# A hybrid two-layer model on one core: the RWKV-7 recurrence in four chunks of 64 steps instead of two of 128

## The chip, the cores and the metric

The kernel runs on one core of one Trainium2 chip. The metric is the device time of one execution in microseconds (us), of which the median of several runs is taken. All arithmetic is fp32. Engines: PE (TensorE matmul; PEld is its weight load), DVE (VectorE), ACT (ScalarE), POOL (GpSimd), SP (SyncE, which here only issues DMAs).

## The reference, cut to what matters

256 tokens of width 1024 pass an even layer (RG-LRU and RWKV-7 side by side, then an FFN), an odd layer (mLSTM, then a mixture of 8 experts) and a final norm. The change lies in the RWKV-7 part, with 8 heads of 64:

```python
def step(state, inp):
    r_t, w_t, k_t, v_t, kk_t, a_t = inp
    sa = einsum('bhvk,bhk->bhv', state, -kk_t)
    state = (state * w_t[:, :, None, :] + sa[..., None] * (kk_t * a_t)[:, :, None, :]
             + v_t[..., None] * k_t[:, :, None, :])
    return state, einsum('bhvk,bhk->bhv', state, r_t)
```

It also moves parts of the RG-LRU (a conv of width 4, two sigmoid gates, tanh and square root, a linear scan) which is computed beside it.

## The kernel before, in words

The order on every engine is written out by hand; engines wait on counting semaphores. The projections of layer 0 come as 11 pairs of 128 columns, `project(0)` to `project(10)`, 32 matmuls of 128x128x256 in records of two per product, into PSUM banks 0 to 3 in turn; each waits until ACT (`shifted`, or copies of lru_x and the gate) and DVE (`shift`) have emptied its bank. Between them stand small groups on PE: `z_done` (decay), `kk_sum` (norm of k), `am_done` (a), `g_done` (gate).

The recurrence is chunked: for each chunk and head the steps of a chunk are related by a triangular matrix, whose inverse is built by doubling. The head dimension is 64, so a group of 128 rows of a tile `j` (four of them) holds two heads; `q` counts chunk and head parity, so that (q, j) are the 16 pairs of chunk and head. In order on PE:

- `transposed`: V, then the LRU's gate products, then B and K, turned through PE and emptied by ACT.
- pairwise products: for each q, K and B (64 rows of 128) against AR (A and R side by side, 256 columns), and A against B: 48 products. DVE masks them into NR, RBt, XT, X and M.
- levels 1 to 6: Z = M XT for each (q, j), ACT empties Z, then X Z and Z X; DVE merges both into XT and X by a masked copy (`copy_predicated`, L1364 and L1367). All tiles 128x128. After each level DVE does one part of the LRU (`lru(lv)`, L1343 to L1358).
- chunk steps: values (nv), U, state ST, output y; chunk 1 waits for the state of chunk 0.

Then `project_out` begins with the LRU's half of the output projection, followed by the layer norm of y. `Em` and `Ep` are decay factors, from scans of `sg` (Gp), by 16 exponentials on ACT. Constants: `cf` (fp32 matrices) gates the first matmul, `lm` (masks, loaded as fp32 and cast by POOL). The FFN weights are fetched once y is done.

## Time and profile before

| | us |
|---|---|
| median of 3 runs | 1499.72 (1496.15 to 1500.17) |
| the profiled execution | 1502.07 |
| its span, first to last instruction | 1500.3 |
| PE busy, share of the span | 1418.1 (95%) |
| PEld busy | 887.5 (59%) |
| DVE, ACT busy | 326.2 (22%), 181.1 (12%) |

A profile records one execution. A busy PE is not a PE at its peak, for its records overlap and its clock has two levels: the granted clock (PEclk) is 1.00 at 2.4 GHz and 0.50 at 1.2 GHz. In shapes, "64*128 64x256" is a matmul that uses 64 rows and 128 columns of the array, with a moving operand of 64 partitions by 256 columns. The chain of work that ended last is what sets the time; a share on it says little about what a part would give if it were shorter, since another wait may end later.

### The profile page before, as it was taken

What the parts mean: (1) busy time and instruction counts of PE and PEld (TensorE: products, weight loads), DVE (VectorE), ACT (ScalarE), POOL (GpSimd) and SP (SyncE); (2) the same over time, 40 slices, a digit from 0 to 9 for tenths busy, and PEclk for the clock granted to TensorE, in tenths of its full rate; (3) what the DMA queues carried; (4) which work ended last, traced back from release to release, by engine and by line L of the source; (5) the groups of instructions that cost most, each with busy time, mean ns of one, the idle gap of its engine ahead of it and who ended that gap; (6) DMA issues with size and microseconds to landing.
All of it is one profiled execution on the core that took longest, in us unless ns stands there. A gap on an engine that the chain in (4) does not pass through costs nothing.

```text
span 1500.3 us, 25303 instructions
## 1 busy us (share of the span) xinstructions
PE 1418.1 (95%) x11796; PEld 887.5 (59%) x11796; DVE 326.2 (22%) x603; ACT 181.1 (12%) x380; POOL 12.9 (1%) x23
## 2 busy tenths in 40 slices
PE   6999999899999989979799999999999999999995
PEld 5787996688888868758454344343443434434332
DVE  2364650500000062484200000010100101001012
ACT  2242211100000023230111000000000000000001
POOL 0010000000000000000000000000000000000000
PEclk9995996999999999798899999999999999999998
DMA  9400000593610270324378999999999999999742
GB/s 361 162 0 0 1 2 0 188 349 128 219 43 1 84 298 13 141 116 176 110 287 325 388 396 361 402 376 391 391 360 395 369 398 386 371 392 359 299 151 91
DMA packets 72913, 348.03 MB, mean 232 GB/s; under 512 B 5720, under 2 KB 13144, under 8 KB 56160
## 3 DMA queue, kind: packets, MB, share of 16 engines
q1 hardware_dynamic: 72496, 345.33, 59.4%
q8 instruction: 94, 1.54, 0.4%
q10 hardware_dynamic: 304, 1.00, 0.2%
q14 instruction: 19, 0.16, 0.0%
HBM read 345.26 MB, written 1.05 MB: 231 GB/s over the span
## 4 chain that ended last, share of the span: by engine, by line
PE 89%; DVE 4%; DMA 3%; ACT 2%; issue 1%; DVEq 0%; SPq 0%; ACTq 0%
PE ps L460 89%; DMA W<-in_moe 3%; DMA cf<-in_cf 1%; DVE rs L1235 1%; DVE W L1344 0%; DVE S L1442 0%; DVE xn L1237 0%; ACT xn L960 0%; PE ps L813 0%; DVE W L1474 0%; DVE W L1384 0%; DVE W L1364 0%; ACT W L1040 0%; DVE W L1367 0%; ACT W L1033 0%
## 5 line engine op out<-in xcount | busy, mean ns | idle before, releaser
L460 PE MATMUL ps<-W,S 128*32 128x352 f32 (+2 forms) x8352 | 701.9, 491 | 9.3 <-DMA W<-in_moe 7.3
L460 PEld LDWEIGHTS ps<-W,S 128*32 128x32 f32 (+1 forms) x8352 | 279.0, 111 | 422.3 <-issue 391.6
L460 PE MATMUL ps<-xn,W 128*128 128x256 f32 (+1 forms) x1600 | 359.3, 385 | 13.0 <-DVE xn L1237 9.0
L460 PEld LDWEIGHTS ps<-xn,W 128*128 128x128 f32 (+1 forms) x1600 | 304.9, 191 | 65.2 <-issue 14.7
L460 PE MATMUL ps<-S,W 128*128 128x256 f32 (+5 forms) x616 | 151.5, 392 | 10.5 <-issue 3.1
L1535 DVE TENSOR_TENSOR S<-S,ps 128x352 f32<-128x352 f32 x48 | 25.0, 521 | 592.4 <-ACT S L1172 589.1
L460 PEld LDWEIGHTS ps<-S,W 128*128 128x128 f32 (+3 forms) x616 | 114.5, 195 | 47.3 <-issue 28.1
L460 PE MATMUL ps<-W 128*128 128x128 f32 (+4 forms) x752 | 101.9, 303 | 4.3 <-DVE W L1337 1.4
L460 PEld LDWEIGHTS ps<-W 128*128 128x128 f32 (+1 forms) x752 | 94.1, 205 | 10.3 <-issue 3.1
L1172 ACT ACTIVATE S<-ps 128x352 f32<-128x352 f32 x48 | 20.5, 462 | 546.2 <-PE ps L460 542.5
L1404 DVE TENSOR_TENSOR S<-S,ps 128x256 f32<-128x256 f32 x22 | 9.3, 421 | 206.8 <-ACT S L1088 206.8
L460 PE MATMUL ps<-S 64*128 64x256 f32 (+2 forms) x128 | 38.9, 496 | 1.9 <-ACT W L1033 1.9
L460 PE MATMUL ps<-xn,cf 128*128 128x256 f32 x80 | 22.9, 449 | 18.5 <-DMA cf<-in_cf 10.8
L460 PEld LDWEIGHTS ps<-S 64*128 64x128 f32 (+1 forms) x128 | 31.8, 301 | 7.5 <-issue 2.2
L1180 ACT ACTIVATE W<-ps 64x512 f32<-64x512 f32 x32 | 18.9, 591 | 137.4 <-PE ps L460 137.1
L1524 DVE TENSOR_TENSOR x<-x,ps 128x1024 f32<-128x1024 f32 x16 | 19.5, 1221 | 71.4 <-PE ps L460 71.4
L1088 ACT ACTIVATE S<-ps 128x256 f32<-128x256 f32 x22 | 8.4, 383 | 210.9 <-PE ps L460 210.9
L460 PEld LDWEIGHTS ps<-xn,cf 128*128 128x128 f32 x80 | 17.8, 229 | 23.1 <-DMA cf<-in_cf 10.8
L1542 DVE STREAM_TRANSPOSE S<-S 128x352 f32<-128x352 f32 x48 | 26.2, 545 | 15.1 <-PE ps L460 11.4
L460 PE MATMUL ps<-S,xn 128*128 128x288 f32 (+1 forms) x96 | 23.0, 401 | 2.2 <-DVE S L1513 1.9
L1056 ACT ACTIVATE W<-ps 128x512 f32<-128x512 f32 x24 | 14.3, 597 | 76.0 <-PE ps L460 76.0
L960 ACT ACTIVATE xn<-x 128x256 f32<-128x256 f32 x40 | 13.0, 405 | 77.6 <-PE ps L460 51.1
(210 smaller groups left out, 471.8 us busy)
## 6 DMA issues: line engine op xcount, KB each, us to landing
W<-in_moe SPq DMA_DIRECT2D x128, 1408.0 KB, 8.3
W<-in_moe SPq DMA_DIRECT2D x176, 512.0 KB, 6.4
W<-in_l_ffn_w SPq DMA_DIRECT2D x12, 2048.0 KB, 10.8
W<-in_l_w_in SPq DMA_DIRECT2D x5, 2048.0 KB, 21.1
W<-in_l_ffn_w SPq DMA_DIRECT2D x6, 1536.0 KB, 12.8
W<-in_l_w_out SPq DMA_DIRECT2D x2, 4096.0 KB, 27.9
W<-in_l_w_in SPq DMA_DIRECT2D x2, 4096.0 KB, 22.5
W<-in_wqkv SPq DMA_DIRECT2D x1, 1536.0 KB, 18.4
```

The lines of the kernel that those rows point to most:

```text
L460: return nc.tensor.matmul(o, l, r, start=start, stop=stop, **kw)
L960: A_(xn[:, k, :], x[:, k, :], ACT.Square).then_inc(sq_done, 1)
L1056: A_(Z[:, q].rearrange("p j t -> p (j t)"), ps[:, q, :], ACT.Copy).then_inc(zcp, 1)
L1088: A_(sil0[:, f % 4, :], ps[:, 4 + f % 4, 0:T], ACT.Silu).then_inc(silu_done, 1)
L1172: A_(sil[:, i % 2, :], ps[:, 2 * t, 0:QN], ACT.Silu).then_inc(m_silu, 1)
L1180: ins = A_(ye[64 * b2:64 * b2 + 64, 512 * i:512 * (i + 1)], ps[64 * i:64 * i + 64, 6 + b2, :], ACT.Copy)
L1235: step(V.reciprocal(rs[:, :], rs[:, :]))
L1404: V.tensor_tensor(hid0[:, f % 4, :], sil0[:, f % 4, :], ps[:, 4 + f % 4, T:2 * T], ALU.mult).then_inc(hid_done, 1)
L1524: V.tensor_tensor(x[:, 4 * r:4 * r + 4, :].rearrange("p d t -> p (d t)"), x[:, 4 * r:4 * r + 4, :].rearrange("p d t -> p (d t)"), ps[:, 2 ...
L1535: V.tensor_tensor(hid, sil[:, i % 2, :], ps[:, 2 * t + 1, 0:QN], ALU.mult).then_inc(m_hid, 1)
L1542: V.transpose(hidT[:, h, t, :], hid).then_inc(m_ht, 1)
```

## The change

The chunk becomes L = 64 steps, of which there are NC = 4, and the levels are five (LV = 6, from 1) instead of six. The products of the recurrence use 64x64 tiles: two chunks (u = 0, 1) lie in the two halves of the partitions, so q and j now stand for a pair of chunks, a head parity and a tile. For each level M is masked before the product (ML, one matrix per level, by POOL), so that the level's results are added by PE, DVE (Z + identity) and a plain copy of XT and X together on ACT (XX) instead of masked copies. The pairwise products, six groups `pair(0)` to `pair(5)`, stand between projections 7, 8 and 9; the LRU's gate products stand before the last projection. The blocks of the weight are fetched in another order, with lru_x before r. The sigmoid of the decay comes after the second projection instead of behind the fifth; Gp is centred on DVE, after which two wide exponentials replace sixteen. POOL scales B and K for the state. The masks are loaded as bytes. Gelu is applied in the fourth level. The values of all chunks are computed ahead, as are the parts of state and y that need no U; then four steps follow, each with state, U, new state and y.

```diff
-LV = 7
+L = 64
+NC = T // L
+LV = 6
...
-        WIN_BLOCKS = [(20, 2), (12, 4), (8, 4), (16, 4), (0, 4), (4, 4)]
+        WIN_BLOCKS = [(20, 2), (12, 4), (8, 4), (0, 4), (16, 4), (4, 4)]
...
+            pool.wait_ge(proj, 1)
+            nc.gpsimd.tensor_copy(XX[:, :, :, :, :].rearrange("p q x j t -> p (q x j) t"),
+                                  con(EYE, n=L).unsqueeze(1).broadcast_to([P, 32, L])).then_inc(xt_init, 1)
+            pool.wait_ge(e_done, 2)
...
+            for src, dst in ((Bm, Bs), (Kt, Ks)):
+                nc.gpsimd.tensor_tensor(dst.rearrange("p j (c t) -> p (j c) t", c=NC), src[:, :, :].rearrange("p j (c t) -> p (j c) t", c=NC),
+                                        DSC.rearrange("p j c -> p (j c)").unsqueeze(2).broadcast_to([P, 4 * NC, L]), ALU.mult).then_inc(scaled, 1)
+            pool.wait_ge(m_raw, 2)
+            for lv in range(2, LV):
+                nc.gpsimd.tensor_tensor(ML[:, lv - 1].rearrange("p q j t -> p (q j) t"), M[:, :, :, :].rearrange("p q j t -> p (q j) t"),
+                                        con(LOW + (lv - 1) * L, n=L).unsqueeze(1).broadcast_to([P, 16, L]), ALU.mult).then_inc(low_done, 1)
...
+            def pair(i):
+                c2, kind = divmod(i, 3)
+                b0 = 4 + 2 * (i % 2)
+                if i >= 2:
+                    pe.wait_ge(pair_out, i - 1)
+                if i == 4:
+                    pe.wait_ge(m_raw, 1)
+                for j in range(4):
+                    for u in range(2):
+                        for par in range(2):
+                            h, c = half(par), 2 * c2 + u
+                            t = slice(c * L, (c + 1) * L)
+                            if kind < 2:
+                                ins = mm(ps[half(u), b0 + par, j * P:(j + 1) * P], (Kt, Bm)[kind][h, j, t],
+                                         AR[h, j, c, :, :].rearrange("p a t -> p (a t)"), True, True)
+                            else:
+                                ins = mm(ps[half(u), b0 + par, j * L:(j + 1) * L], AR[h, j, c, 0, :], Bm[h, j, t], True, True)
+                ins.then_inc(pair_done, 1)
...
-            for i in range(7, 11):
-                project(i)
-
+            project(5)
+            project(6)
+            project(7)
+            pe.wait_ge(ops_done, 1)
+            pe.wait_ge(a_done, 1)
+            pe.wait_ge(g_out, 1)
+            pair(0)
+            pair(1)
+            project(8)
+            pair(2)
+            pair(3)
+            project(9)
+            pair(4)
+            pair(5)
+            pe.wait_ge(conv0, 1)
+            for turn in range(10, 14):
+                lru_gate(turn)
+            project(14)
 
...
+            pe.wait_ge(pair_out, 5)
+            transposed(0, v_)
+            pe.wait_ge(scaled, 2)
+            pe.wait_ge(pair_out, 6)
+            pe.wait_ge(m_raw, 2)
+            transposed(1, Bs)
+            pe.wait_ge(tr_out, 2)
+            transposed(2, Ks)
+
             for lv in range(1, LV):
+                if lv > 1:
+                    pe.wait_ge(low_done, lv - 1)
                 for q in range(4):
-                    if lv > 1:
+                    if lv == 1:
+                        drained((12, 13, 14, 11)[q])
+                    else:
                         pe.wait_ge(xcp, 4 * (lv - 2) + q + 1)
                     for j in range(4):
-                        ins = mm(ps[:, q, j * P:(j + 1) * P], M[:, q, j, :], XT[:, q, j, :], True, True)
+                        for u in range(2):
+                            ins = mm(ps[half(u), q, j * L:(j + 1) * L], ML[half(u), lv - 1, q, j, :], XX[half(u), q, 0, j, :], True, True)
                     ins.then_inc(zmm, 1)
+                if lv == 1:
+                    pe.wait_ge(tr_out, 6)
                 for q in range(4):
                     pe.wait_ge(zcp, 4 * (lv - 1) + q + 1)
                     for j in range(4):
-                        ins = mm(ps[:, 4 + q, j * P:(j + 1) * P], X[:, q, j, :], Z[:, q, j, :], True, True)
+                        for u in range(2):
+                            ins = mm(ps[half(u), 4 + q, j * L:(j + 1) * L], XX[half(u), q, 1, j, :], Z[half(u), q, j, :], True, True)
                     if lv < LV - 1:
                         for j in range(4):
-                            ins = mm(ps[:, q, j * P:(j + 1) * P], Z[:, q, j, :], X[:, q, j, :], True, True)
+                            for u in range(2):
+                                ins = mm(ps[half(u), 4 + q, T + j * L:T + (j + 1) * L], Z[half(u), q, j, :], XX[half(u), q, 1, j, :], True, True)
                     ins.then_inc(xmm, 1)
...
+            def cols(c2, j):
+                return slice(c2 * T + j * L, c2 * T + (j + 1) * L)
+
+            def values_in(c2):
+                for j in range(4):
+                    for u in range(2):
+                        for par in range(2):
+                            ins = mm(ps[half(u), par, cols(c2, j)], NR[half(u), 2 * c2 + par, j, 0, :], Vt[half(u), c2, j, half(par)],
+                                     c2 == 0 and j == 0, c2 == 0 and u == 0, skip_group_check=True)
+                return ins
+
+            values_in(0)
+            values_in(1).then_inc(nv_done, 1)
+            pe.wait_ge(xcp, 4 * (LV - 1))
+            for c in range(NC):
+                c2, u = divmod(c, 2)
+                hu = half(u)
+                if c:
+                    pe.wait_ge(st_out, c)
+                    for j in range(4):
+                        for par in range(2):
+                            h = half(par)
+                            ins = mm(ps[hu, par, cols(c2, j)], AR[h, j, c, 0, :], ST[h, c - 1, j, :], False, True, skip_group_check=True)
+                    ins.then_inc(nv_done, 1)
+                    for j in range(4):
+                        for par in range(2):
+                            h = half(par)
+                            mm(ps[h, 6 + u, cols(c2, j)], ST[h, c - 1, j, :], AR[h, j, c, 1, :], False, False, skip_group_check=True)
+                pe.wait_ge(nv_out, 2 * c + 2)
                 for par in range(2):
                     for j in range(4):
-                        h, q = half(par), 2 * c + par
-                        o = ps[h, 4 + 2 * par + c, j * P:(j + 1) * P]
-                        mm(o, Vt[:, c, j, h], NR[:, q, j, 1, :], True, False)
-                        ins = mm(o, U[:, c, 2 * j + par, :], RBt[:, q, j, :], False, c == 0)
-                        if c == 1:
-                            ins = mm(o, ST[h, j, :], AR[h, c, j, 1, :], False, True)
+                        ins = mm(ps[hu, 2 + par, cols(c2, j)], XX[hu, 2 * c2 + par, 0, j, :], RHS[hu, c2, par, j, :], True, True)
+                    ins.then_inc(u_done, 1)
+                if c == 0:
+                    for cb in range(NC - 1):
+                        b2, bu = divmod(cb, 2)
+                        for j in range(4):
+                            for par in range(2):
+                                mm(ps[half(par), 4 + bu, cols(b2, j)], Ktk[half(bu), b2, j, half(par)], Vt[half(bu), b2, j, half(par)],
+                                   b2 == 0 and j == 0, False, skip_group_check=True)
+                    for b2 in range(CH):
+                        for j in range(4):
+                            for bu in range(2):
+                                for par in range(2):
+                                    mm(ps[half(par), 6 + bu, cols(b2, j)], Vt[half(bu), b2, j, half(par)], NR[half(bu), 2 * b2 + par, j, 1, :],
+                                       b2 == 0 and j == 0, False, skip_group_check=True)
+                pe.wait_ge(u_out, 2 * c + 2)
+                if c < NC - 1:
+                    for j in range(4):
+                        for par in range(2):
+                            ins = mm(ps[half(par), 4 + u, cols(c2, j)], Bt[hu, c2, j, half(par)], U[hu, c2, par, j, :], False, True, skip_group_check=True)
+                    ins.then_inc(st_done, 1)
+                for j in range(4):
+                    for par in range(2):
+                        ins = mm(ps[half(par), 6 + u, cols(c2, j)], U[hu, c2, par, j, :], RBt[hu, 2 * c2 + par, j, :], False, True, skip_group_check=True)
                 ins.then_inc(y_done, 1)
 
...
+            shifted(7)
+            shifted(8)
+
+            def m_copy(c2):
+                act.wait_ge(pair_out, 3 * c2 + 3)
+                for par in range(2):
+                    ins = A_(M[:, 2 * c2 + par].rearrange("p j t -> p (j t)"), ps[:, 4 + 2 * c2 + par, 0:T], ACT.Copy)
+                ins.then_inc(m_raw, 1)
+
+            m_copy(0)
...
+            def pair(i):
+                c2, kind = divmod(i, 3)
+                dve.wait_ge(pair_done, i + 1)
+                for par in range(2):
+                    q, src = 2 * c2 + par, ps[:, 4 + 2 * (i % 2) + par, :]
+                    wide = src.rearrange("p (j a t) -> p j a t", j=4, a=2)
+                    narrow = src[:, 0:T].rearrange("p (j t) -> p j t", j=4)
+                    if kind == 0:
+                        ins = V.tensor_tensor(NR[:, q].rearrange("p j a t -> p j (a t)"), src.rearrange("p (j n) -> p j n", j=4),
+                                              con(MASKS).unsqueeze(1).broadcast_to([P, 4, P]), ALU.mult)
+                    elif kind == 1:
+                        V.tensor_tensor(RBt[:, q], wide[:, :, 1, :], con(MASKS + L, n=L).unsqueeze(1).broadcast_to([P, 4, L]), ALU.mult)
+                        ins = V.copy_predicated(XX[:, q, 0], lm[:, 0:L].unsqueeze(1).broadcast_to([P, 4, L]), wide[:, :, 0, :])
+                    else:
+                        V.copy_predicated(XX[:, q, 1], lm[:, L:2 * L].unsqueeze(1).broadcast_to([P, 4, L]), narrow)
+                        ins = V.tensor_tensor(ML[:, 0, q], narrow, con(LOW, n=L).unsqueeze(1).broadcast_to([P, 4, L]), ALU.mult)
+                ins.then_inc(pair_out, 1)
...
 
-                if part == 1:
-                    dve.wait_ge(lroot, 1)
-                    step(V.tensor_scalar(lt[:, :, :], lt[:, :, :], 1.0, None, ALU.add))
-                    step(V.reciprocal(lt[:, :, :], lt[:, :, :]))
-                if part == 2:
+                if part in (2, 3):
+                    if part == 2:
+                        dve.wait_ge(lroot, 1)
+                        step(V.tensor_scalar(lt[:, :, :], lt[:, :, :], 1.0, None, ALU.add))
+                    j0 = slice(2 * part - 4, 2 * part - 2)
+                    step(V.reciprocal(lt[:, j0, :], lt[:, j0, :]))
+                if part == 4:
                     step(V.scalar_tensor_tensor(lr[:, :, :], lr[:, :, :], 2.0, lt[:, :, :], ALU.mult, ALU.mult))
                     V.memset(lr[:, :, 0:1], 1.0)
                     step(V.tensor_scalar(lt[:, :, :], lt[:, :, :], 2.0, -1.0, ALU.mult, ALU.add))
...
+                    dve.wait_ge(zmm, 4 * (lv - 1) + q + 1)
+                    V.tensor_tensor(Z[:, q], ps[:, q, 0:T].rearrange("p (j t) -> p j t", j=4),
+                                    con(EYE, n=L).unsqueeze(1).broadcast_to([P, 4, L]), ALU.add).then_inc(zcp, 1)
                 lru(lv)
```

## Rows read from the trace of the kernel before

**Rows 1.** The page: PE and its clock in 40 slices, the chain, a group

```profile
PE   6999999899999989979799999999999999999995
...
PEclk9995996999999999798899999999999999999998
...
PE 89%; DVE 4%; DMA 3%; ACT 2%; issue 1%; DVEq 0%; SPq 0%; ACTq 0%
...
L460 PE MATMUL ps<-W,S 128*32 128x352 f32 (+2 forms) x8352 | 701.9, 491 | 9.3 <-DMA W<-in_moe 7.3
```

**Rows 2.** Chain in order of time: start us, us, what

```profile
116.76 31.21 PE ps L460 x90
...
165.28 6.56 DVE W L1344
```

**Rows 3.** PE's timeline: start us, us, engine, line, operation, tiles, shapes

```profile
19.94 23.87 PE L460 MATMUL ps<-xn,W 128*128 128x256 f32 x96 [3.04 <-DVE xn L1237]
...
63.18 1.99 PE L460 MATMUL ps<-S,W 64*128 64x256 f32 x8 [1.72 <-ACT W L997]
...
80.74 27.79 PE L460 MATMUL ps<-xn,W 128*128 128x256 f32 x128
...
116.76 31.20 PE L460 MATMUL ps<-S 64*128 64x256 f32 x96 [1.95 <-ACT W L1033]
149.35 66.21 PE L460 MATMUL ps<-W 128*128 128x128 f32 x560 [1.39 <-DVE W L1337]
...
237.71 1.11 PE L460 MATMUL ps<-W 128*64 128x128 f32 x4 [0.69 <-ACT W L1070]
238.75 0.69 PE L460 MATMUL ps<-S,W 64*64 64x128 f32 x2
...
250.99 5.46 PE L460 MATMUL ps<-xn,W 128*128 128x256 f32 x16
```

**Rows 4.** Windows (us, PE, PEld, DVE, ACT, POOL busy, PEclk, DMA, GB/s); group by form

```profile
112.00:116.00 4.00, 2.81 (x21) 2.40 (x20) 0.00 (x0) 3.98 (x11) 0.00 (x0) 1.00 0.00 0
120.00:124.00 4.00, 4.00 (x16) 3.44 (x16) 1.94 (x6) 0.57 (x1) 0.00 (x0) 0.50 0.02 4
144.00:148.00 4.00, 3.96 (x14) 3.20 (x12) 1.60 (x5) 0.00 (x0) 0.00 (x0) 0.50 0.00 0
...
220.00:224.00 4.00, 4.00 (x44) 4.00 (x45) 0.42 (x1) 0.00 (x0) 0.00 (x0) 0.52 0.00 0
244.00:248.00 4.00, 4.00 (x16) 2.35 (x16) 0.00 (x0) 0.00 (x0) 0.00 (x0) 0.50 0.00 0
...
L460 PE MATMUL ps<-W 128*64 128x64 f32 x32 | 2.0, 319 | 0.7 <-ACT W L1070 0.7
```

**Rows 5.** Window inside the levels, PE alone

```profile
157.00:176.00 19.00, 19.00 (x171) 1.00 0.01 2
```

**Rows 6.** DMA issues of the two constant tables

```profile
S<-in_lm ACTq DMA_DIRECT2D x1, 896.0 KB
cf<-in_cf SPq DMA_DIRECT2D x1, 705.0 KB, 9.6
```

**Rows 7.** DVE, ACT and Pool by line and form, layer 0 (Pool: all)

```profile
L1284 DVE RECIPROCAL W<-W 128x1024 f32<-128x1024 f32 x1 | 6.6, 6553 | 0.0
...
L1325 DVE TENSOR_TENSOR W<-ps,cf 128x512 f32<-128x512 f32 x8 | 5.2, 685 | 19.6 <-PE ps L460 19.6
...
L1331 DVE TENSOR_TENSOR W<-ps,cf 128x256 f32<-128x256 f32 x8 | 3.4, 420 | 8.4 <-PE ps L460 8.4
...
L1056 ACT ACTIVATE W<-ps 128x512 f32<-128x512 f32 x24 | 14.3, 597 | 76.0 <-PE ps L460 76.0
...
L1051 ACT ACT_TABLE_LOAD x1 | 1.3, 1283 | 0.0
...
L454 POOL TENSOR_TENSOR S<-S,cf 128x256 f32<-128x256 f32 x8 | 5.8, 726 | 119.7 <-ACT S L1123 119.7
```

More of the change, by code:

```diff
@@ L306, in hybrid_rglru_rwkv7_mlstm_moe @@
         block = ctx.enter_context(nc.Block())
+        TURNS = [("project", i) for i in range(10)] + [("gate", i) for i in range(4)] + [("project", 10)]
         PAIRS = []
@@ L990, in _ @@
             shifted(1)
+            act.wait_ge(z_done, 1)
+            for j in range(4):
+                ins = A_(sg[:, j, :], ps[:, 6 + j // 2, (j % 2) * T:(j % 2 + 1) * T], ACT.Sigmoid, bias=col("l0_w0", j))
+            ins.then_inc(sg_done, 1)
             shifted(2)
```

440 lines of the change are left out of this document (183 added, 257 removed).

## The prediction

> **What bounds the kernel now.** The page first: PE is busy in nearly every slice and the chain that ended last runs through it for 89% of the span [rows 1]. So what counts is what PE does and at which clock. The change touches only the RWKV recurrence of layer 0 and the projections around it; the chain in order of time [rows 2] and PE's own timeline [rows 3] show where that lies. 19.94 to 108.5 us: eleven projection pairs, 6.9 us each at full clock (27.79 us for four), with one stall of 1.72 us before 63.18. 108.5 to 116.7: transposes, LRU gates, transposes, with 1.95 us idle. 116.76 to 149.35: the pairwise products, 48 matmuls that take 31.2 us. 149.35 to 215.6: six levels, 272 matmuls of 128x128x128; here PE is full except that at 165.28 a reciprocal of 6.56 us on DVE holds the chain, with PE's queue filled from other quarters. 215.6 to 251.0: the two chunk steps, with handovers to ACT and short matmuls. At 250.99 the output projection begins. Nothing after that depends on the form of the recurrence, so the forecast is a new date for that moment.
>
> The reader is to see the clock next. In the pairwise products PE is busy 4.00 of 4.00 us and is still granted 0.50 from 120 on, where each matmul uses 64 of 128 rows; before them, at 112 to 116, it had idled. In the levels (all rows, all columns) it gets 1.00, in the second chunk step (64 output columns at a time) 0.50 again [rows 4]. So the 31.2 us are 10,240 columns at 3.05 ns, about 4 cycles of 1.2 GHz a column.
>
> **Prices.** A product is two records. In the levels 171 records take 19.00 us [rows 5]: 111 ns a record, 222 ns a product of 128 columns at 2.4 GHz; a product of 64 columns by itself then costs about 107 ns at 2.4 and 213 at 1.2 GHz. Can two half-size products run together? The state products of the first chunk (64 output columns, alternating column halves) are 16 products in 2.0 us; less the last one's own 0.32 that is 106 ns each, at clock 0.50 [rows 4, 5]: half of 213. So two column tiles do overlap, at the low clock. Four tiles of 32 columns do so in the experts: 8,352 records of 352 or 512 columns at 84 ns [rows 1]. Two tiles that differ in row half and column half (the form of the new levels) are not in this trace. Bounds: 107 ns (full overlap) and 213 ns (none) at 1.2 GHz, half that at 2.4 as a floor. I take 107, since the nearest row is the 106.
>
> The Trainium skill has a rule against this: TensorEngine Tiling, section Restrictions and Gotchas, says that different row tiles can't access the same PSUM bank at once. The new levels write both row tiles into one bank, on different partitions. By the rule they would run one after another; no run so far shows it, and that is rival B.
>
> **The change, part by part**, against the profiled execution's own 1502.07 us (span 1500.3; the median of three is 1499.72, so 2.35 less).
>
> 1. Start. The table in_lm shrinks from 896 KB to some 16 KB and cf grows from 705 to about 900 KB [rows 6]. PE starts at 10.85, on cf. Some 0.7 MB less lies ahead of it; ACT's squares, which begin when x lands, then are next. Between 0 and 2.5 us; I take 1 gained.
>
> 2. Projections and early work. Eleven projections remain, at 6.9. The sigmoid behind the 1.72 us stall no longer waits for the fifth projection: gained. From 19.94, eight projections (9.8 for the first at low clock, 7 x 6.9) and the four small groups (7.4) end near 86. DVE must have ops_done by then: the square root ends near 57, then 0.7 + 6.55 (the reciprocal, [rows 7]) + 1.2, shift, one subtraction of 1,040 columns (1.25), two wide exponentials and a table load on ACT (3.5), four products of 1.22: about 78.5. It holds with 7 us of slack; were that cover gone, every us late is a us lost.
>
> 3. Pairwise products. 64 products of 128 columns and 32 of 64, in four tiles (2 row halves x 2 column halves, row halves in separate banks). At full clock with four together: 64 x 213/4 + 32 x 107/4 ns = 4.3 us; none together 17.1. DVE's evictions (0.42 for 256 columns, 0.69 for 512, [rows 7]), some 10 us for the six groups, lie beside projections 8 and 9 (13.8 us). Behind the last two groups they do not: DVE needs about 4.5 us after PE's 103, ACT copies M only then (its sigmoids for the LRU gates are queued behind that copy, with a table load of 1.28 us), and projection 10 waits for the first gate eviction: a new stall of about 2.6 us. Pool's two scalings of 1,024 columns (0.73 us for 256, so some 2.9 each) start at 78.5 and end in time; its four mask products need 11.6 us from 108 on, one is due per level from the second: in time. Then gates 3.5, the last projection 6.9, 24 transposes with evictions between them 3: levels start near 120, with 1 us more for the shape changes of the array (2 records of 64*64 start 1.04 us after 4 records of 128*64 worth 0.85, [rows 3]; ten such changes). So 121 in the place of 149.35: 28.3 gained, of which the products are some 27.
>
> 4. Levels. Now five, each 32 + 64 products of 64 columns (the last 32 + 32): 448. At 107 ns: 10.3 us a level, 6.8 the last: 47.8. DVE evicts Z (0.42 for 256 columns) and ACT both X (0.60 for 512, [rows 7]); both are under PE's 0.86 and 1.7 us a quarter at this clock. But Z's eviction now sits behind the LRU parts on DVE, and the reciprocal part waits for ACT's tanh and square root, which ACT does between levels: in the third level DVE is free about 7.3 us after the level starts (last copy 0.9, table and root 2.3, add 0.7, half reciprocal 3.4) where PE wants it at 3.4: 4.4 us lost. Sum 52.7 for 66.3: 13.5 gained.
>
> Which clock? Two diagonal 64x64 tiles fill half the array, as the 64-row products at 120 to 148 do, and those stayed at 0.50 with PE full. I take 0.50.
>
> The page TensorE: Matmul & The Clock Gate of the Trainium skill (Part 1, the two states) ties the 2.4 GHz to a busy engine; rows 4 show a fully busy engine at 1.2, so the measurement decides against the rule as it is worded. By the rule the levels would run at 2.4: rival A.
>
> 5. Four chunk steps. 32 products for the values (3.4 us), eviction 0.4, U of the first chunk (8 in one tile, not overlapped: 1.7), 56 products that fill the wait (6.0), state (0.85 + 0.3 + 0.45 for DVE): 13.4. Each of the next two: products with the state 1.7, U 1.7 + 0.7, state 1.6: 5.7. The last 5.3, with the y products. Sum 29.9 for 35.4: 5.5 gained. The LRU product now follows on DVE and is done about when y is: 0 to 1.2 lost, I take 0.
>
> Sum: 1 + 28.3 + 13.5 + 5.5 = 48.3; 1502.07 - 48.3 = 1453.8, against the median 1451.4.
>
> **Rivals.** A: the clock stays at 1.00 through levels and steps. For: the levels start from a full clock behind a projection, and both row halves and both column halves are in use. Against: half the array is. Levels: 23.9 of work; the waits on DVE in the third grow to 6.1 and ACT and DVE add some 2.5: 32.5. Steps 17.5. Another 32.6 gained: 1419 against the median. If records can't follow faster than the 53 ns seen, most of this gain is absent.
>
> B: diagonal tiles into one bank do not overlap, others do. Levels 95.6 + 1, values 3.4 and state products 2.6 more: 49.9 lost again, 1501.
>
> C, the other side: no two of the 64x64 tiles overlap. Pairs 12.8 more, levels 43.9, steps 18 (224 products at 213 ns are 47.7): 74.7 lost, 1526, slower than before. It decides from the point at which two thirds of the overlap (48.3 of 74.7) is missing. Against it: the 106 ns; for it: that row tiles share the moving-data path in a way no row shows.
>
> D: the work between the projections isn't hidden (DVE late, a stall before each pair group, the clock lost in the 2.6 us stall and regained one projection later): 5 to 15 us, 1457 to 1466. This is inside the main case's own range, 1432 to 1474, together with products of 64 columns at up to 140 ns (448 x 33 ns = 15 us).
>
> **How the numbers follow.** Main case 0.66, A 0.20, B 0.06, C 0.06, and 0.02 that nothing moves. The range goes down to A's neighbourhood, 1415, and up to 1476; B and C stay out, with a little at either end. A measurement of this kernel can tell about 0.3% (4.5 us) from no change: faster 0.90, same 0.04, slower 0.06.
>
> **What would show it.** Right: the output projection starts near 202; the levels last 50 to 55 us at 0.50, with one gap near the third; pair groups last under 1 us. Wrong: clock 1.00 in the levels (A); 17 us or more a level (B, C); PE gaps over 3 us before the first pair group (step 2). A span that shrinks by another amount than the date of the output projection would mean that something after it was touched, which I hold to be nothing.

## The result, and the profile after the change

The changed kernel takes 1428.51 us (median of four, 1423.0 to 1436.62), the kernel before 1499.81 us beside it (median of four, 1496.15 to 1500.17). The ratio is 0.953, with a 95% interval of 0.9504 to 0.9555. The forecast was 1451; the range held the result only because it reached down towards rival A; the case that I had called likeliest did not occur. The profiled execution of the changed kernel took 1430.38 us with a span of 1428.4, where the one of before has 1502.07 and 1500.3.

The page of the kernel after: busy tenths of PE, its granted clock, and the shares of the chain, to be held against [rows 1].

```profile
PE   6998889999998999787999999999999999999995
...
PEclk9999999999999995988999999999999999999998
...
PE 89%; DVE 4%; DMA 4%; ACT 2%; issue 1%; DVEq 0%; SPq 0%; ACTq 0%
```

PE is still the engine that the chain runs through. A slice is now 35.7 us long, so the levels and chunk steps lie in the fourth and fifth; the dip of the clock to 5 in the sixteenth is not in the part that was changed, and will matter below.

PE's own timeline of the kernel after: start us, us, line, operation, tiles, shapes, count of records, and the idle time before it with its releaser. It answers to [rows 3].

```profile
8.64 5.12 PE L473 MATMUL ps<-xn,cf 128*128 128x256 f32 x16 [8.64 <-DMA cf<-in_cf]
16.79 14.05 PE L473 MATMUL ps<-xn,W 128*128 128x256 f32 x64 [3.04 <-DVE xn L1277]
...
79.89 1.98 PE L473 MATMUL ps<-S 64*64 64x128 f32 x64
81.80 7.17 PE L473 MATMUL ps<-xn,W 128*128 128x256 f32 x32
88.91 1.57 PE L473 MATMUL ps<-S 64*64 64x64 f32 x64
...
104.39 7.17 PE L473 MATMUL ps<-xn,W 128*128 128x256 f32 x32 [1.66 <-ACT S L1079]
...
114.32 13.28 PE L473 MATMUL ps<-W 64*64 64x64 f32 x448
133.37 17.19 PE L473 MATMUL ps<-W 64*64 64x64 f32 x512 [5.77 <-DVE W L1408]
151.45 4.04 PE L473 MATMUL ps<-W 64*64 64x64 f32 x160 [0.90 <-DVE W L1415]
...
168.11 5.38 PE L473 MATMUL ps<-xn,W 128*128 128x256 f32 x16 [0.67 <-DVE xn L1403]
```

The output projection starts at 168.11 in the place of 250.99. That is 82.9 us earlier, and the span is only 71.9 shorter. The pair groups (two at a time, 1.6 to 2.0 us) sit between projections of 7.17 with no idle time ahead of them. The levels begin at 114.32. Their records with the values' are 448 + 512 = 960; of these the last 64 are the values', which take 1.9 us at 29 ns a record, so the levels end near 148.6.

Windows of the kernel after: us, then busy us and count of PE, PEld, DVE, ACT and POOL, granted clock, DMA share, GB/s. The first six answer to [rows 4, 5]; the last two lie in the mLSTM stage, far behind the change.

```profile
116.00:120.00 4.00, 4.00 (x144) 4.00 (x142) 1.96 (x3) 1.79 (x3) 0.00 (x0) 1.00 0.01 4
124.00:128.00 4.00, 3.60 (x124) 3.46 (x120) 0.00 (x0) 3.30 (x5) 0.00 (x0) 1.00 0.02 4
128.00:132.00 4.00, 0.00 (x0) 0.00 (x0) 3.19 (x2) 0.74 (x1) 0.00 (x0) 0.87 0.00 0
132.00:136.00 4.00, 2.63 (x50) 2.63 (x52) 3.97 (x6) 0.60 (x1) 0.00 (x0) 0.50 0.01 4
136.00:140.00 4.00, 4.00 (x114) 4.00 (x114) 1.68 (x2) 1.82 (x4) 0.00 (x0) 0.78 0.00 0
140.00:144.00 4.00, 4.00 (x146) 4.00 (x142) 3.38 (x7) 3.39 (x4) 0.00 (x0) 1.00 0.01 4
...
545.00:560.00 15.00, 14.38 (x48) 10.85 (x47) 7.77 (x19) 1.69 (x7) 1.22 (x2) 0.50 0.00 0
560.00:575.00 15.00, 13.54 (x56) 10.81 (x57) 8.90 (x19) 3.23 (x11) 1.85 (x3) 0.62 0.00 1
```

Two things are to be read here. At the start of the levels the clock is 1.00, and 448 records take 13.28 us in PE's timeline, the last one's own 0.22 included: 29 ns a record, 58 ns a product of two records. (The count of a window takes in the records that reach into it from either side, so 144 in 4.00 us are some eight too many.) So the diagonal tiles overlap, and at 2.4 GHz. Then the chain of waits passes from PE to ACT and DVE and PE has nothing for 5.77 us. The clock falls to 0.50 within that gap, at 131, and is back at 1.00 at 137.8, within the window of 136 to 140, 4.4 us after PE has started again.

The chain in order of time through that gap: start us, us, engine and line.

```profile
125.78 0.60 ACT W L1104
...
127.69 1.06 ACT S L1097
...
128.78 0.70 DVE W L1386
...
129.50 3.36 DVE W L1388
...
132.89 0.44 DVE W L1408
...
133.37 13.43 PE ps L473 x384
```

It is the square root on ACT (127.69), the addition and the half reciprocal on DVE (128.78 and 129.50), and only then the eviction of Z that PE wants: the stall that step 4 of the prediction named, at the size that rival A gave it.

Where the time went, from dates of PE's timeline in the two kernels:

| part | before | after | gained | forecast |
|---|---|---|---|---|
| to the first projection | 19.94 | 16.79 | 3.2 | 1 |
| first projection to levels | 129.4 | 97.5 | 31.9 | 28.3 |
| levels | 66.2 | 34.3 | 31.9 | 13.5 |
| values, steps, to the output projection | 35.4 | 19.5 | 16.0 | 5.5 |
| LayerNorms and FFN, to the mLSTM stage | 275.5 | 275.4 | 0.1 | 0 |
| mLSTM stage | 171.9 | 181.9 | -10.0 | 0 |
| rest (experts above all) | | | -1.1 | 0 |

The sum is 72.0, the difference of the spans 71.9. The 66.2 of before are counted as in the prediction and hold the values of its first chunk, 16 records that take 1.9 us; without them the levels took 64.3. The mLSTM stage runs the same instructions in both kernels; in this execution its clock is 0.50 from 530 to 571.

### The profile page after: what moved, and what is told of

It reads as the page before. It is cut to its first block, busy times and chain, and to the rows that moved or that the text cites. A ratio compares the mean times of both kernels' runs of the same rounds, so it can differ in the third digit from the quotient of the medians.

```text
span 1428.4 us, 26690 instructions
## 1 busy us (share of the span) xinstructions
PE 1343.4 (94%) x12500; PEld 822.2 (58%) x12500; DVE 301.6 (21%) x588; ACT 179.4 (13%) x368; POOL 19.1 (1%) x21
## 4 chain that ended last, share of the span: by engine, by line
PE 89%; DVE 4%; DMA 4%; ACT 2%; issue 1%; DVEq 0%; SPq 0%; ACTq 0%
PE ps L473 88%; DMA W<-in_moe 3%; DVE rs L1275 1%; DMA cf<-in_cf 1%; DVE S L1495 0%; DVE xn L1277 0%; ACT xn L1005 0%; PE ps L858 0%; DVE W L1527 0%; DVE W L1437 0%; DVE W L1388 0%; PE ps L539 0%; DVE W L1399 0%; ACT rs L1013 0%; ACT xn L1185 0%
## 5 line engine op out<-in xcount | busy, mean ns | idle before, releaser
L473 PE MATMUL ps<-W 64*64 64x64 f32 (+2 forms) x1296 | 53.4, 232 | 8.6 <-DVE W L1408 5.8
L473 PEld LDWEIGHTS ps<-W 64*64 64x64 f32 (+1 forms) x1296 | 49.3, 145 | 11.9 <-DVE W L1408 5.9
L1577 DVE TENSOR_TENSOR x<-x,ps 128x1024 f32<-128x1024 f32 x16 | 19.5, 1221 | 71.4 <-PE ps L473 71.4
L473 PEld LDWEIGHTS ps<-S,xn 128*128 128x128 f32 x96 | 18.9, 208 | 6.3 <-issue 3.1
L473 PE MATMUL ps<-S,cf 128*128 128x128 f32 (+1 forms) x44 | 14.4, 473 | 3.6 <-DVE xn L1496 3.6
L1277 DVE SCALAR_TENSOR_TENSOR xn<-x,vec,rs 128x256 f32<-128x256 f32 x40 | 16.3, 479 | 0.2
## 6 DMA issues: line engine op xcount, KB each, us to landing
W<-in_l_ffn_w SPq DMA_DIRECT2D x6, 1536.0 KB, 13.5
```

The lines of the kernel that those rows point to most:

```text
L473: return nc.tensor.matmul(o, l, r, start=start, stop=stop, **kw)
L1277: V.scalar_tensor_tensor(dst[:, k, :], x[:, k, :], col(name, k), rs[:, :], ALU.mult, ALU.mult).then_inc(xn_done, 1)
L1577: V.tensor_tensor(x[:, 4 * r:4 * r + 4, :].rearrange("p d t -> p (d t)"), x[:, 4 * r:4 * r + 4, :].rearrange("p d t -> p (d t)"), ps[:, 2 ...
```

## Experiments

Four questions: does the change itself take the 10 us in the mLSTM stage? What are the pair products and the place of their groups worth? Why did the clock stay up where I took it to be low? And what is the gap in the third level worth?

| kernel | median us (lowest to highest, n) | ratio (95%) |
|---|---|---|
| again | 1424.94 (1423.36 to 1439.15, 4) | 0.9513 (0.9452 to 0.9575) |
| early | 1423.5 (1417.38 to 1428.29, 4) | 0.9464 (0.942 to 0.9509) |
| bpairs | 1485.43 (1484.61 to 1488.27, 4) | 0.9894 (0.9861 to 0.9928) |
| before, beside these three | 1502.0 (1497.77 to 1507.5, 7) | |
| late | 1430.8 (1427.55 to 1443.5, 4) | 0.955 (0.9502 to 0.9597) |
| best | 1412.02 (1407.61 to 1434.21, 6) | 0.9412 (0.9387 to 0.9438) |
| before, beside these two | 1501.56 (1493.05 to 1506.21, 11) | |

rowhalf, colhalf, onetile, bestrow and bestgap were executed once each, with a profile; they are read by dates in the trace, not by their time.

### again: the changed kernel once more, unchanged

> The changed kernel, once more. In its first profile the output projection began at 168.1 us, 82.9 earlier than before, yet the span shrank by 71.9: the mLSTM stage (439 to 625 us) took 10 us longer, with the clock at 0.50 from about 531 to 572. Theory 1 (the low clock there is a matter of where the chip's clock stands when the stage begins, not of the change): the start of the output projection stays within 1 us of 168.1 and the loss in the mLSTM stage varies, between 0 and 12 us. Theory 2 (the change causes it): the stage takes 10 us longer again, to 1 us.

Its output projection starts at 168.55 (168.11 before), so the part that was changed repeats within half a microsecond. The mLSTM stage took 174.7 us and not 181.9. Windows of it, same columns as above:

```profile
545.00:560.00 15.00, 13.88 (x56) 11.16 (x57) 10.24 (x22) 3.17 (x11) 1.91 (x3) 0.61 0.00 1
560.00:575.00 15.00, 13.20 (x78) 10.22 (x77) 11.98 (x25) 3.33 (x12) 1.90 (x3) 0.95 0.00 0
```

The same instructions are at 0.61 and 0.95 here where the first profile has 0.50 and 0.62. In the profiles of the changed kernel and its variants the stage took 167.1 to 183.5 us, and the longest one (bestrow) and the shortest (best and colhalf) have the same code there. So the 7 us between these two executions are not the change's. The old form took 171.9 us in both of its profiles (before and bpairs, whose code is the same there), in the lower half of that range; two profiles don't show that the change had no part at all in the rest.

### bpairs: the kernel before, with only the order of its pair products changed

```diff
-            for q in range(4):
-                c, h = q // 2, half(q % 2)
+            for c in range(CH):
                 for left in (Kt, Bm):
-                    banks = claim(2)
+                    banks = claim(4)
                     for j in range(4):
-                        ins = mm(ps[:, banks[j // 2], (j % 2) * T:(j % 2 + 1) * T], left[h, c, j, :],
-                                 AR[h, c, j, :, :].rearrange("p a t -> p (a t)"), True, True)
+                        for par in range(2):
+                            h = half(par)
+                            ins = mm(ps[:, banks[2 * par + j // 2], (j % 2) * T:(j % 2 + 1) * T], left[h, c, j, :],
+                                     AR[h, c, j, :, :].rearrange("p a t -> p (a t)"), True, True)
```

> The kernel before with one part alone: its pairwise products (64 rows, 128 columns) alternate between the row halves instead of doing four of one half after the other. Theory (tiles of different row halves overlap, and with both halves in use the clock stays or returns to 1.00): the phase shrinks from 32.6 us to DVE's own eviction time, 8.9 us a chunk, so 17 to 20 us, and the median by 12 to 15 us. Rival 1 (they overlap but the clock stays at 0.50): 17 to 19 us too, with PE near 17.1 and the clock at 0.50. Rival 2 (no overlap between row halves): the phase stays at 31 to 33 us.

The median falls by 16.6 us. From the first pair product to the levels it is 18.1 us (117.10 to 135.20) where before has 32.6 [rows 3]. Its windows:

```profile
118.00:122.00 4.00, 4.00 (x25) 3.81 (x24) 2.25 (x4) 2.87 (x4) 0.00 (x0) 0.57 0.02 4
122.00:126.00 4.00, 3.37 (x38) 2.67 (x34) 3.69 (x11) 0.00 (x0) 0.00 (x0) 1.00 0.00 0
126.00:130.00 4.00, 2.28 (x26) 2.07 (x26) 4.00 (x7) 0.00 (x0) 0.00 (x0) 1.00 0.00 0
```

Before has PE full at 0.50 in this stretch [rows 4]; here both row halves are in use in turn, the clock is back at 1.00 in 122 to 126, and DVE is the engine that is full. So 14.5 of the 32.6 us that the products cost in the kernel before were missing overlap and a low clock, and what was left is bounded by DVE's evictions. In the changed kernel these lie beside the projections. The phase is as long as expected (17 to 20), and the median fell by a little more than expected (12 to 15). The clock falls here too, at 118.4 where before has 118.0, although both row halves are in use; what is new is that it comes back after 3.4 us.

### late: the pair groups moved behind projections 8 and 9

```diff
+            project(8)
+            project(9)
             pair(0)
             pair(1)
-            project(8)
             pair(2)
             pair(3)
-            project(9)
             pair(4)
             pair(5)
```

> The changed kernel with its six pair groups after projections 8 and 9 instead of between them, DVE's order unchanged. Theory (the placement hides DVE's evictions and conv, about 14.7 us from the first group to the last): PE idles 8 to 11 us between the pair groups, the output projection begins 7 to 11 us later relative to the first projection, and the median rises by 7 to 14 us. Rival (what counts is the four tiles, and the placement is worth little because PE waits for the last eviction in both): under 3 us.

PE's timeline of late shows what the projections had covered:

```profile
96.88 0.69 PE L473 MATMUL ps<-S 64*64 64x64 f32 x32 [0.64 <-DVE W L1355]
...
103.11 2.84 PE L473 MATMUL ps<-S 64*64 64x128 f32 x64 [3.78 <-ACT W L1068]
...
111.80 7.17 PE L473 MATMUL ps<-xn,W 128*128 128x256 f32 x32 [0.97 <-ACT S L1079]
```

From the first projection to the levels it is 104.4 us and not 97.5: 6.8 us later, just under the 7 to 11 expected. PE idles 6.3 us from the pair groups to the last projection where I had 8 to 11 between the groups, and the changed kernel has 1.66; some 2 us more are the clock, which is 0.50 from 101 to 108. The medians are 2.3 us (against the first measurement of after) and 5.9 us (against again) apart, below the 7 to 14 that I had expected, and the intervals of the ratios overlap. So the place of the groups is worth about 7 us by the trace, which rules out the rival (under 3), and the medians of four runs don't resolve it; the forecast for them was missed.

### rowhalf, colhalf, onetile: which part of the array the levels use

All three keep the number, the size and the order of the levels' products. The first takes both factors from one row half only (that of the even chunk), the second writes to one column half only, the third uses a single 64x64 tile. All three leave out the inverse of the odd chunks. One product stands for the three of each; in colhalf two waits of PE are moved as well, since the odd chunks' products go to other banks:

In rowhalf:

```diff
-            ins = mm(ps[half(u), q, j * L:(j + 1) * L], ML[half(u), lv - 1, q, j, :], XX[half(u), q, 0, j, :], True, True)
+            ins = mm(ps[half(u), q, j * L:(j + 1) * L], ML[half(0), lv - 1, q, j, :], XX[half(0), q, 0, j, :], True, True)
```

In colhalf:

```diff
-            ins = mm(ps[half(u), q, j * L:(j + 1) * L], ML[half(u), lv - 1, q, j, :], XX[half(u), q, 0, j, :], True, True)
+            ins = mm(ps[half(0), q + 4 * u, j * L:(j + 1) * L], ML[half(u), lv - 1, q, j, :], XX[half(u), q, 0, j, :], True, True)
```

In onetile:

```diff
-            ins = mm(ps[half(u), q, j * L:(j + 1) * L], ML[half(u), lv - 1, q, j, :], XX[half(u), q, 0, j, :], True, True)
+            ins = mm(ps[half(0), q, j * L:(j + 1) * L], ML[half(0), lv - 1, q, j, :], XX[half(0), q, 0, j, :], True, True)
```

> The changed kernel with the products of the levels all taken from the upper row half: every second product (odd chunks) reads the operands of the first, and still writes its own column half; the inverse of the odd chunks is thereby left out. As many products in as many tiles, but one row half. Theory R (what kept the clock is that both row halves run): records still follow at 27 ns at first (column tiles overlap), but after the gap behind level 2 the clock stays at 0.50, so that levels 3 to 5 take about 27 us instead of 13.4 plus what follows. Theory C (any two tiles that overlap will do): the clock returns to 1.00 during level 3, as in the changed kernel, and the levels last 37 us.

> The changed kernel with all products of the levels written to the lower column half, while their operands still come from both row halves; those of the odd chunks go to another bank, so the odd chunks' inverse is left out. The mirror of the run on one row half, in which the clock stayed at 0.50 from 132 to 170 us and the output projection began at 181.9. Theory R (both row halves running is what brings the clock back): overlap as before, the clock returns to 1.00 between 136 and 142, levels end near 151.5, the output projection begins within 2 us of 168. Theory D (it takes both halves of rows and of columns): the clock stays at 0.50 after the gap, levels 3 to 5 take 27 us, the output projection begins near 182.

> The changed kernel with all products of the levels on one 64x64 tile (rows and columns of the even chunk, each done twice in the place of the odd one's), so that nothing can overlap; the inverse of the odd chunks is left out. It measures the price without overlap. By the prediction's price: 213 ns a product at 0.50 and 107 at 1.00; 448 products, 96 us if the clock stays at 0.50, 48 to 55 with 1.00. Theory: the clock falls and the levels last 85 to 97 us, output projection at 215 to 228. Rival (a product costs less than its columns say, since records of one tile are pipelined): under 75 us.

Windows of rowhalf:

```profile
116.00:120.00 4.00, 4.00 (x145) 4.00 (x141) 2.43 (x5) 1.39 (x3) 0.00 (x0) 1.00 0.01 4
136.00:140.00 4.00, 4.00 (x82) 4.00 (x80) 2.13 (x1) 1.74 (x3) 0.00 (x0) 0.50 0.00 0
152.00:156.00 4.00, 4.00 (x82) 4.00 (x80) 2.55 (x5) 0.38 (x1) 0.00 (x0) 0.50 0.02 4
```

Windows of colhalf:

```profile
136.00:140.00 4.00, 1.33 (x24) 1.33 (x26) 3.96 (x6) 0.00 (x0) 0.00 (x0) 0.61 0.00 0
140.00:144.00 4.00, 4.00 (x85) 4.00 (x84) 2.87 (x1) 1.21 (x3) 0.00 (x0) 0.54 0.02 4
144.00:148.00 4.00, 4.00 (x144) 4.00 (x142) 2.46 (x5) 3.63 (x5) 0.00 (x0) 1.00 0.02 4
```

Windows of onetile:

```profile
118.00:126.00 8.00, 8.00 (x141) 8.00 (x140) 1.71 (x3) 1.79 (x3) 0.00 (x0) 1.00 0.01 2
136.00:140.00 4.00, 4.00 (x73) 4.00 (x71) 0.00 (x0) 2.70 (x4) 0.00 (x0) 1.00 0.00 0
160.00:170.00 10.00, 10.00 (x97) 10.00 (x96) 3.51 (x7) 2.42 (x3) 0.00 (x0) 0.50 0.01 2
...
196.00:200.00 4.00, 3.33 (x136) 3.17 (x134) 0.83 (x2) 0.76 (x2) 0.00 (x0) 0.94 0.01 4
```

Read the clock column, each time ahead of and behind the gap in the third level. Ahead of it all three are at 1.00, onetile for 27 us with a quarter of the array. Behind it colhalf, which uses both row halves, is back at 1.00 in 144 to 148; rowhalf, with one row half, stays at 0.50 with PE full for all of its levels 3 to 5 (133.9 to 158), and onetile likewise (144.9 to 193). Behind the levels come the values, which use both row halves in all three kernels: in onetile the clock is back at 196.5, 3.7 us after they begin; in rowhalf at 169.7, 11.8 us after they begin, with a gap of 0.67 us and the products of U in one tile between. The output projection starts at 174.11 in colhalf (54.5 us from the start of its levels, 53.8 in the changed kernel; the 168 expected was missed because the levels themselves began 5.3 us later, 3 of them from a first projection at the low clock), at 181.94 in rowhalf and at 213.77 in onetile. So in these executions, one of each, one row half does not bring the clock down; it keeps it from coming back.

The same runs price the overlap. rowhalf and colhalf pass as many records in 4.00 us as the diagonal tiles do (145 and 144), two at a time. The single tile takes 58 to 59 ns a record with nothing overlapped at 1.00 (448 in 26.34 us), and 107 ns at 0.50; rowhalf, overlapped at 0.50, takes 53 ns.

My expectation for onetile, levels of 85 to 97 us, was missed: they took 78, because I had the clock low from the start and it held for 27 us. The rival's 75 us was missed too.

### early: the gap in the third level taken away

ACT's tanh and square root go ahead of the levels (the buffer lt moves to a free place), and DVE's LRU work is spread so that only half reciprocals stand in the second and third parts.

```diff
-        lt = view(W, XB + 7168, "p (j t) -> p j t", j=4, t=T)
+        lt = view(W, XB + 3072, "p (j t) -> p j t", j=4, t=T)
...
+            for j in range(4):
+                ins = A_(lt[:, j, :], lr[:, j, :], ACT.Tanh, scale=SP4[:, j:j + 1])
+            ins.then_inc(lth, 1)
             act.wait_ge(proj, 11)
...
-                if lv == 3:
+                if lv == 1:
                     act.wait_ge(lth, 1)
```

> Tanh of the LRU before the last projection's copy, square root before level 1, reciprocal halves in levels 2 and 3, one product moved from level 5 to 4. Theory: the 7.6 us between the end of level 2's products (125.8) and level 3's (133.4) are the wait for tanh, square root, addition and half reciprocal in a row; after it the clock is at 0.50 until about 139, another 3 us. Then the levels end 8 to 12 us earlier and the median falls by as much. Rival: ACT and DVE are simply full in the levels (five levels of about 5.1 us of PE work against 1.7 + 3.4 us of DVE), and the work moved comes back as gaps of 1 to 2 us in each level: gain under 4 us.

PE's timeline of early has the levels and the values in one piece:

```profile
117.11 28.26 PE L473 MATMUL ps<-W 64*64 64x64 f32 x960
```

The changed kernel takes 36.2 us for the same records (114.32 to 150.56): 28.3, the gap of 5.77, and 2.2 for the clock behind it. But the windows of early show that the clock fell later instead, in the chunk steps:

```profile
148.00:152.00 4.00, 3.81 (x146) 3.53 (x142) 1.28 (x3) 0.38 (x1) 0.00 (x0) 1.00 0.02 4
152.00:156.00 4.00, 3.42 (x74) 3.15 (x73) 1.69 (x4) 0.76 (x2) 0.00 (x0) 0.77 0.00 0
156.00:160.00 4.00, 3.49 (x48) 3.30 (x47) 0.78 (x2) 0.38 (x1) 0.00 (x0) 0.50 0.02 4
```

The levels and values are 8.0 us shorter, the low end of the 8 to 12 expected, and no gaps of 1 to 2 us took the gap's place, so the rival is out. But from the first projection to the output projection it is 147.6 us, in again 151.4: only 3.8 gained. 1.4 of the difference is the first projection, which ran partly at 0.50 in this execution (15.47 us for 14.05), and the rest is the low clock in the chunk steps. The median fell by 1.4 to 5.0 us and not by 8 to 12. That the gap goes when ACT's functions come early and DVE's parts are spread is shown (the two were moved together); its price was not there to be had in full in this execution.

### best: early, with ACT's gates ahead of a copy and the last LRU part inside the first chunk step

```diff
-            m_copy(1)
             for i in range(4):
...
                 ins.then_inc(lgate_out, 1)
+            m_copy(1)
...
+                if c == 0:
+                    lru(6)
...
-            lru(6)
```

> The kernel of the early square root, with two more moves: ACT empties the LRU gates before it copies M, and the LRU's last product is done by DVE in the first chunk step's wait instead of after the last. Theory: the 1.66 us stall before the last projection and the 0.23 to 0.67 us before the output projection go, 2 us together; from the first projection to the output projection 145.5 us where the early kernel took 147.6, and the changed kernel 151.3 (at like clock). The median is 3 to 8 us under the changed kernel's 1428.5. Rival: M's copy is late for Pool's masks (7.9 us in the trace) and level 2 or 3 waits for them instead: no gain over the early kernel.

PE's timeline of best:

```profile
105.50 7.07 PE L473 MATMUL ps<-xn,W 128*128 128x256 f32 x32
...
115.32 28.26 PE L473 MATMUL ps<-W 64*64 64x64 f32 x960
144.25 4.04 PE L473 MATMUL ps<-W 64*64 64x64 f32 x160 [0.67 <-DVE W L1413]
...
160.44 3.72 PE L473 MATMUL ps<-xn,W 128*128 128x256 f32 x16
```

The idle time before the last projection is gone (1.66 in the changed kernel), and so is the gap in the levels; from 21 us on the clock stays at 1.00 to the output projection, 142.1 us after the first projection (expected 145.5, 151.3 in the changed kernel). At 1412.02 us it is 89.5 us under the kernel before on its chip, and its interval lies below that of the changed kernel: it beats both. Five of its six executions took 1407.61 to 1414.64 us, one 1434.21. The median is 12.9 to 16.5 us under the changed kernel's two, where I had expected 3 to 8; the trace shows 9.2 of that in the changed part, and the rest is not explained by the edit (the mLSTM stage of this profile was the shortest but one).

### bestrow and bestgap: the gap and the row half, each by itself

bestrow is best with the edit of rowhalf: one row half, but no gap. bestgap is best with a gap put back, by two half reciprocals more on DVE ahead of the third level, of which the second undoes the first:

```diff
             for lv in range(1, LV):
+                if lv == 3:
+                    step(V.reciprocal(lt[:, 0:2, :], lt[:, 0:2, :]))
+                    step(V.reciprocal(lt[:, 0:2, :], lt[:, 0:2, :]))
```

> The best kernel (no gap in the levels: 960 records in 28.3 us) with the products of the levels taken from the upper row half only, as in the run on one row half; the inverse of the odd chunks is left out. Theory G (a granted clock of 1.00 falls only behind a gap; the halves in use decide whether it comes back): the clock stays at 1.00 through all five levels, which last 28 to 29 us. Theory F (use of one row half by itself lowers the clock): it falls within the levels, as it would in 28 us of such work, and they last 35 to 50 us.

> The best kernel with a wait put back: two extra reciprocals on DVE (3.35 us each, the second undoes the first) before the evictions of level 3, so that PE idles some 6 us there. Theory G: the clock falls to 0.50 behind the gap and, since both row halves run, comes back after 5 to 8 us: the levels last 28.3 + 6 for the gap + 2 to 4 for the low clock, 36 to 39 us. Rival (the gap alone costs, the clock stays): 34 to 35 us.

Windows of bestrow:

```profile
136.00:140.00 4.00, 4.00 (x143) 4.00 (x141) 3.58 (x8) 1.93 (x5) 0.00 (x0) 1.00 0.02 4
```

Windows of bestgap:

```profile
128.00:132.00 4.00, 0.89 (x16) 0.89 (x18) 3.96 (x6) 0.00 (x0) 0.00 (x0) 0.87 0.00 0
132.00:136.00 4.00, 4.00 (x106) 4.00 (x104) 3.31 (x2) 1.54 (x3) 0.00 (x0) 0.70 0.02 4
136.00:140.00 4.00, 4.00 (x146) 4.00 (x142) 2.79 (x5) 3.64 (x5) 0.00 (x0) 1.00 0.02 4
```

Without a gap one row half costs nothing: bestrow passes the levels at 1.00 throughout, 960 records in 28.26 us, the same as best. With a gap of 5.42 us bestgap falls and is back in 136 to 140, and its levels and values take 35.4 us: 28.3, the 5.4 of the gap, and 1.7 for the clock. I had expected 36 to 39, so the gap itself, not the low clock behind it, is the larger part of its price. The low clock lasted 3.4 us here and 6.8 in the changed kernel. The cases together, in the levels:

| | no gap | a gap of 3.9 to 5.8 us |
|---|---|---|
| both row halves | 1.00 throughout (early, best) | falls, back at 1.00 within two windows of 4 us (after, colhalf, bestgap) |
| one row half | 1.00 throughout (bestrow) | falls and stays at 0.50 (rowhalf, onetile) |

This holds for the levels and is not a rule for all work, as the kernel before shows. In its chunk steps PE has no idle time from 219.97 to 232.6, and the clock falls all the same, at 230.6 (in bpairs, with the same code there, at 214.0, PE without idle time from 203.5). Its windows:

```profile
228.00:230.00 2.00, 2.00 (x13) 1.59 (x12) 0.00 (x0) 0.00 (x0) 0.00 (x0) 1.00 0.00 0
230.00:232.00 2.00, 2.00 (x10) 1.63 (x9) 0.00 (x0) 0.00 (x0) 0.00 (x0) 0.66 0.00 0
```

And it then stays at 0.50 with PE full from 237.7 to 251.0, in products of which two thirds use all 128 rows, and all only 64 columns at a time [rows 3, 4], until 3.6 us into the output projection. Nor does a gap decide by itself: the same 3.04 us ahead of the first projection were followed by a low clock in before, bpairs, early, best and colhalf, and not in the other seven profiles; the 1.66 us ahead of the last projection never were.

## Why the prediction was right or wrong, step by step

**Start (step 1): right in kind.** 1 us was forecast from 0 to 2.5. PE starts on cf at 8.64 in the place of 10.85 (2.2 earlier), and the first projection 3.2 earlier. Beyond that the first projection ran at clock 1.00, where before shows 0.50 until 25.8: 6.9 us for 9.8, which stands in the second row of the table above. This part is luck and not the change: early, best and colhalf, which start alike, lost 1.4, 1.4 and 3.0 us of it to the low clock.

**Projections and pair products (steps 2 and 3): right.** No gap ahead of the first pair group, so DVE's 7 us of slack held; the groups last 1.6 to 2.0 us by twos between projections, and the last projection waits 1.66 us where I had 2.6. The 3.6 us over the forecast are the 2.9 of the first projection's clock and the smaller stall, less small change. bpairs shows 16.6 us of the gain by itself in the old form, late shows some 7 for the place.

**Levels (step 4): the step that failed is its clock.** The count (448 products) and the overlap were right: at 0.50 a product takes 107 ns (rowhalf), as forecast, and at 1.00 it takes 58, a little over half. What failed is the sentence "I take 0.50". I had read the pair products of [rows 4] as a clock that work on 64 rows brings down. It came down 1.2 us into them, behind 1.95 us without work, and did so in bpairs too, where both row halves are in use; what one row half did was to keep it from coming back. In the levels bestrow (no gap, one row half, 1.00) against rowhalf (gap, one row half, 0.50 to the end of its levels) shows this, and that the levels use both row halves is why they came back behind their gap (colhalf, bestgap). With the clock right the same working gives rival A, 32.5 us for the levels. They took 34.3: 26.3 of work (as in best; A had 23.9), the stall of 5.77 (6.1 by A, 4.4 in the main case) and some 2 of low clock behind it, which A did not have; A's 2.5 for ACT and DVE did not occur.

**Chunk steps (step 5): the same step failed.** 29.9 us were forecast at 0.50, 17.5 by A, and 19.5 measured. A middle step takes 4.13 us (from the state products at 158.49, which wait for U, to those at 162.62), where half of PE's part in my working (1.7 + 1.7 + 1.6, so 2.5) and the 0.7 of the eviction give 3.2. PE is busy for 3.44 of the 4.13, so I had PE's part too small and the handovers about right (0.69, of which 0.52 behind DVE).

**The sum.** Levels and steps together: 53.8 us measured, 82.6 forecast, 50.0 by rival A. The output projection was to start near 202 and starts at 168.1. That the forecast missed by 22 us and not by 34 is no merit of it: about 10 us came back in the mLSTM stage. Two sums of the working are slightly off their terms: 47.8 + 4.4 is 52.2 where step 4 has 52.7, and the first chunk step's terms give 13.1 where step 5 has 13.4.

**"Nothing after that depends on the form of the recurrence": true of the work, not of the clock.** The stages up to the mLSTM are alike to 0.1 us. The mLSTM stage took 181.9 us against 171.9, and 174.7 in the second execution of the same kernel. The prediction's last sentence would have taken this difference as a sign of an edit there, and that reading would have been wrong.

**Rivals.** A held for the changed part. B is out: the diagonal tiles pass as many records as tiles in one bank and different column halves (rowhalf) or tiles in different banks (colhalf). B's rule, that different row tiles can't access one PSUM bank at once (the Trainium skill, TensorEngine Tiling, section Restrictions and Gotchas), is not what the trace shows when the two write to different partitions of it: 144 records in 4.00 us, as many as without a shared bank. C is out by onetile, which is C made real in the levels: 58 ns a record at 1.00 against 29. D was small: one stall of 1.66 us.

The rule that I had weighed against [rows 4], that a busy engine gets the 2.4 GHz (the Trainium skill, TensorE: Matmul & The Clock Gate, Part 1), fits after, colhalf and bestgap, and does not fit rowhalf, with PE 4.00 of 4.00 us busy at 0.50 in 136 to 140, nor the kernel before at 230.6. I had thrown the rule out as a whole on such rows; it gave the right clock for this kernel's levels.

**Not settled.** In early the clock fell at 154, in chunk steps whose gaps are about 0.5 us, while best and the changed kernel went through the same steps at 1.00. Why the clock fell in the full chunk steps of before, and which work brings it back there, no run tells; the four cases of the table rest on one or a few executions each. Why the mLSTM stage varies is as open. What the single masked matrix per level brings against masked copies was not tried by itself.

## What to carry to other kernels

Before you price a stage at the clock that similar work had, look at what PE did ahead of that work: a low clock can be left over from a gap, though here it also fell in work without one (the kernel before, at 230.6). Small tiles that alternate between two row halves and two column halves run two at a time even into one bank, and with both row halves in use the clock of the levels came back 3 to 5 us behind the gap, so give PE such pairs and spend the effort on the gap itself (here 5.8 us, which moving ACT's tanh and square root ahead and spreading DVE's work took away). Compare kernels by the date at which the changed part ends, and profile the same kernel twice before you explain a difference in a stage that was not touched.

## What the runs showed of the chip that was not expected

- PE full at clock 0.50 from 133.9 to 158 (rowhalf) and from 144.9 to 193 (onetile), with one row half in use behind a gap; at 1.00 with the work of rowhalf and no gap (bestrow).
- The clock of the kernel before falling at 230.6 us with PE full since 219.97, and so at 214.0 in bpairs.
- Two products of 64x64 tiles in different partitions of one bank overlap fully: 29 ns a record, against 58 ns in a single tile.
- One and the same mLSTM stage took from 167.1 to 183.5 us in different executions, with its clock at 0.50 for up to 48 us on end (bestrow, 521 to 569).
